# First loads of the input projection in eighths on two queues, the norm's broadcast matmuls behind three quarters of a column tile, ScalarE's table loaded ahead

## The chip, the cores and the metric

One core of a Trainium2 chip runs the whole program. The metric is device time in microseconds (us) of one execution, the median over several. TensorE (PE) multiplies matrices into PSUM, VectorE (DVE), ScalarE (ACT) and GpSimd (POOL) work elementwise, SyncE (SP) issues most of the DMAs. All data are f32.

## The reference, cut to what matters

One layer of a decoder for 512 prompt tokens and 8 sample tokens, 520 in all. The change is at its very beginning:

```python
def _rmsnorm(x, g):
    y = x * lax.rsqrt(jnp.mean(x * x, axis=-1, keepdims=True) + EPS) * g
    return y
def _layer(...):
    a = _rmsnorm(h, norm_mix)          # h: 520 x 1024
    proj = a @ w_in                    # w_in: 1024 x 1800: pooling, gate z, x/B/C, dt
    v_pool, z, xbc, dt_raw = proj[..., :o1], proj[..., o1:o2], proj[..., o2:o3], proj[..., o3:]
    pool_out, new_pool = _pool_mixer(v_pool, ...)
    ssd_out, new_conv, new_ssm = _ssd_mixer(z, xbc, dt_raw, ...)
    h = h + concat([pool_out, ssd_out]) @ w_out
    h = h + _hier_moe(_rmsnorm(h, norm_ffn), ...)      # 32 experts, two of them per token
    gate = sigmoid(_rmsnorm(h, norm_ple) @ ple_gate_w + ple_gate_b)
    h = h + gate * (p @ ple_proj_w)
# output: _rmsnorm(h, norm_final), and the new pooling, conv and SSD states
```

## The kernel before

The program is written by hand, engine by engine: each engine's block is a list of instructions in the order in which they run, with semaphore waits (`wait_ge`) between engines. Nothing is scheduled by a tool. `Steps` and `last` are helpers that count an engine's own semaphore.

**The input projection** multiplies the 1024 model dimensions, in 8 slices (k) of 128, by column tiles of 128 outputs. The host has transposed the tokens (`xT`, 128 x 8 x 520) and sorted the columns of `w_in`: `w_a` holds the first four tiles (`A_TILES` 4, 5, 0, 1 of x/B/C), `w_b` dt and two more, `w_v` the pooling tiles, `w_z` the gate's. `aproj(j, k0, k1)` (line 598) is tile j of the first four over some slices: two matmuls per slice, one for each half of the tokens (128x260), so 16 per tile. An f32 matmul stands as two records in the trace (32 per tile). These four tiles start before the norm is known: VectorE only multiplies xT by the norm's gains (line 1551, into `xg`, one instruction per slice, which `aproj(0, ...)` waits for), and the inverse root of each token is multiplied in when the tile leaves PSUM (`take_a`, lines 1567 to 1569).

**The inverse roots** take a path of their own. ScalarE squares and sums the untransposed rows `h1` (line 1116, five tiles of rows, each behind its own load `ld_x`, all behind the constants `ld_const`), GpSimd adds eps and takes the power -0.5 (lines 1405 and 1406, `inverse_root`), VectorE puts the roots on a diagonal (line 1557, `rdiag`), TensorE multiplies ones by it (line 652, five matmuls) so that every partition holds all 520 roots, and VectorE copies them out of PSUM banks 4 and 5 (lines 1559 and 1560, `rstd_b`, semaphore `s_rb_out`). Tile 3 of `aproj` writes the same banks, so it waits for `s_rb_out`.

TensorE's order there is: tiles 0 and 1, slice by slice together as the four quarters land (lines 645 to 648), the five broadcast matmuls, tile 2, tile 3, then dt (`dtproj`, lines 616 and 619), which needs `aT`, the tokens with gain and root in them (line 1585, eight instructions, `s_aT_ready`). Then come the transposes of the sample's conv state and pooling state (line 593 and 667, behind `ld_state`), and tile by tile the rest of the projection (`inproj`, line 633) between the SSD mixer's matmuls. VectorE's order beside that is: `take_a(0)`, `take_a(1)`, `aT`, `take_a(2)`, two convolutions (line 1576), `take_a(3)`, and the chain from the raw dt to its cumulated sums (lines 1595 to 1609, `s_acs_ready`), for which TensorE waits at line 678.

**The loads.** SyncE issues in this order (lines 467 to 494): four times a quarter of xT (two slices, 520 KB) and a quarter of w_a (512 KB), the constants (380 KB), five tiles of `h1` rows, w_b, w_v, w_z, the SSD states, two copies in DRAM. ScalarE issues the vectors (`vec`, 37 KB: gains and biases), GpSimd the two small states (lines 1395 and 1396). Each has a semaphore of its own. The first expert weights are issued by SyncE when the mixer's output is there (`s_mix_ready`, line 516), and later ones as TensorE frees their buffers.

## Time and profile before

| what | value |
|---|---|
| time, median of 3 runs | 569.43 us (569.17, 569.43, 572.87) |
| time of the profiled execution | 570.61 us |
| its span, first to last instruction | 568.8 us |
| mean granted TensorE clock | 0.965 |
| PE busy | 507.8 us (89%) |
| DVE, ACT, POOL busy | 207.7, 154.1, 111.8 us |
| DMA | 144.72 MB, mean 254 GB/s |

Times in the profile are counted from the first instruction. The profiled execution lies 1.8 us around its span, and 1.2 us above the median. An engine that is busy is not for that reason the bound: a row of the waits or of the timeline says, in brackets, how long an engine stood idle before an instruction and which instruction or DMA released it. SPq, ACTq and PEq are the engines' sequencers, which issue DMAs.

### The profile page before, as it was taken

To read this page: it belongs to the slowest core of one execution; us is meant where nothing else is said; L and a number is where in the kernel's file an instruction comes from. 1 tells how busy PE (TensorE), PEld (TensorE's weight loads), DVE (VectorE), ACT (ScalarE), POOL (GpSimd) and SP (SyncE) were. 2 spreads that over 40 slices of the span, in tenths; PEclk is the share of its full clock that TensorE was granted. 3 is DMA by queue.
4 is the path that set the end of the run, shared out by engine and by line. 5 is a ranking of instruction groups with operands and counts; after the bars stand their busy time and mean duration, and the time that the engine had idled before them with its cause. 6 is when DMAs were issued, how large, how long until landed. Compare 5 with 4: busy or idle time off the path is not lost.

```text
span 568.8 us, 7815 instructions
## 1 busy us (share of the span) xinstructions
PE 507.8 (89%) x3098; PEld 312.2 (55%) x3098; DVE 207.7 (37%) x496; ACT 154.1 (27%) x315; POOL 111.8 (20%) x178
## 2 busy tenths in 40 slices
PE   5899999999999997199999999978776999999994
PEld 4688886768645554165555555544343554344443
DVE  1286496523033546432221121111110211169455
ACT  0435163103534121102222222211210223355223
POOL 1200048993001001101121111111011223022001
PEclk9999999999999999579999999999996999999999
DMA  8990000503449705949999999999999999640001
GB/s 290 418 295 3 1 1 10 213 1 68 170 163 400 328 9 199 414 142 341 418 417 415 416 417 416 414 416 417 416 413 382 413 413 365 217 196 39 3 37 74
DMA packets 40214, 144.72 MB, mean 254 GB/s; under 512 B 14522, under 2 KB 15162, under 8 KB 31076
## 3 DMA queue, kind: packets, MB, share of 16 engines
q1 hardware_dynamic: 33316, 132.79, 59.4%
q0 software_dynamic: 5152, 8.85, 4.2%
q10 hardware_dynamic: 1712, 2.62, 1.2%
q8 instruction: 23, 0.38, 0.3%
q14 instruction: 11, 0.09, 0.0%
HBM read 140.15 MB, written 14.19 MB: 271 GB/s over the span
## 4 chain that ended last, share of the span: by engine, by line
PE 44%; DMA 10%; DVE 3%; issue 2%; SPq 2%; ACT 1%; POOLq 0%; POOL 0%; DVEq 0%; ACTq 0%
PE PS L989 18%; PE PS L1092 10%; PE PS L1010 9%; DMA mem<-in_exp_w_down 5%; PE PS L593 4%; DVE mem L1878 2%; DMA u_rows<-mem 2%; DMA mem<-u_rows,idx_all 1%; DMA choice_rows<-mem,out_i 1%; DMA mem<-choice_rows 1%; SPq L484 1%; PE PS L834 1%; SPq L486 1%; PE PS L990 1%; PE PS L996 1%
## 5 line engine op out<-in xcount | busy, mean ns | idle before, releaser
L989 PE MATMUL PS<-mem 128*64 128x256 f32 x512 | 119.3, 387 | 6.8 <-DVE mem L1878 6.8
L990 PE MATMUL PS<-mem 128*64 128x256 f32 x512 | 119.3, 387 | 0.0
L989 PEld LDWEIGHTS PS<-mem 128*64 128x64 f32 x512 | 68.4, 139 | 43.2 <-DVE mem L1878 7.6
L1010 PE MATMUL PS<-mem 128*64 128x512 f32 x256 | 62.6, 610 | 18.1 <-issue 9.0
L633 PE MATMUL PS<-mem 128*128 128x260 f32 x320 | 73.3, 385 | 0.0
L990 PEld LDWEIGHTS PS<-mem 128*64 128x64 f32 x512 | 68.4, 139 | 0.0
L633 PEld LDWEIGHTS PS<-mem 128*128 128x128 f32 x320 | 59.8, 190 | 10.5 <-issue 1.5
L1882 DVE TENSOR_TENSOR mem<-PS,mem 64x256 f32<-64x256 f32 x32 | 13.7, 428 | 119.6 <-ACT mem L1288 119.6
L821 PE MATMUL PS<-mem 128*128 128x512 f32 x128 | 56.6, 595 | 0.0
L1092 PE MATMUL PS<-mem 128*128 128x512 f32 (+1 forms) x144 | 56.1, 547 | 0.0
L593 PEld LDWEIGHTS PS<-mem 128*128 128x128 f32 (+4 forms) x254 | 31.0, 170 | 45.5 <-issue 29.9
L593 PE MATMUL PS<-mem 128*128 128x128 f32 (+4 forms) x254 | 40.0, 289 | 13.5 <-DMA mem<-u_rows,idx_all 12.5
L1878 DVE TENSOR_TENSOR mem<-PS,mem 128x512 f32<-128x512 f32 x34 | 23.5, 692 | 75.3 <-PE PS L593 75.2
L1288 ACT ACTIVATE mem<-PS 64x256 f32<-64x256 f32 x32 | 12.0, 375 | 134.5 <-PE PS L990 134.5
L1010 PEld LDWEIGHTS PS<-mem 128*64 128x64 f32 x256 | 18.4, 139 | 43.6 <-issue 31.6
L1092 PEld LDWEIGHTS PS<-mem 128*128 128x128 f32 x144 | 27.0, 190 | 26.3 <-issue 25.5
L1405 POOL TENSOR_TENSOR mem<-mem 128x1 f32<-128x1 f32 (+1 forms) x20 | 4.5, 225 | 175.9 <-ACT mem L1256 85.2
L821 PEld LDWEIGHTS PS<-mem 128*128 128x128 f32 x128 | 23.8, 190 | 26.9 <-issue 26.8
L604 PE MATMUL PS<-mem 128*128 128x260 f32 x128 | 31.6, 412 | 6.8 <-DMA mem<-in_w_a 6.8
L1293 ACT ACTIVATE mem<-PS 64x512 f32<-64x512 f32 x32 | 18.9, 590 | 65.3 <-PE PS L1010 65.3
L604 PEld LDWEIGHTS PS<-mem 128*128 128x128 f32 x128 | 26.3, 207 | 11.3 <-DMA mem<-in_w_a 6.8
L1483 POOL DMA_INDIRECT mem<-u_rows,idx_all x15 | 15.3, 1021 | 79.4 <-PE PS L593 70.5
(270 smaller groups left out, 547.4 us busy)
## 6 DMA issues: line engine op xcount, KB each, us to landing
mem<-in_exp_w_down SPq DMA_DIRECT2D x32, 1024.0 KB, 21.2
mem<-in_exp_w_gate SPq DMA_DIRECT2D x32, 1024.0 KB, 18.9
mem<-in_exp_w_up SPq DMA_DIRECT2D x32, 1024.0 KB, 22.0
mem<-in_w_out SPq DMA_DIRECT2D x2, 2048.0 KB, 7.4
mem<-in_ple_gate_w SPq DMA_DIRECT2D x1, 4096.0 KB, 29.7
mem<-choice_rows SPq DMA_DIRECT2D x4, 1024.0 KB, 8.8
mem<-in_xT SPq DMA_DIRECT2D x4, 520.0 KB, 9.1
mem<-in_w_a SPq DMA_DIRECT2D x4, 512.0 KB, 9.9
```

What stands on the lines that cost most here:

```text
L593: return pe.transpose(dst, src, ident[0:n, 0:n])
L604: ins = pe.matmul(PS[A_BANKS[j][h]][:, 0:HALF], COLS[j][2][:, k, :], xg[k // 4][:, k % 4, h * HALF:(h + 1) * HALF], start=(k == 0), stop=( ...
L633: ins = pe.matmul(PS[b + h][:, 0:HALF], w[:, k, :], aT[:, k, h * HALF:(h + 1) * HALF], start=(k == 0), stop=(k == KT - 1))
L821: return pe.matmul(PS[OUT_BANKS[i][h]][:, :], mix_col(k, ORDER[i]), w_out[:, k, h * 512:(h + 1) * 512], start=(k == 0), stop=(k == KT - 1))
L989: pe.matmul(PS[0][0:S, 0:FF], rows_k, gu[slot][:, k, :], start=(k == 0), stop=(k == KT - 1))
L990: ins = pe.matmul(PS[1][S:2 * S, 0:FF], rows_k, gu[slot][:, KT + k, :], start=(k == 0), stop=(k == KT - 1))
L1010: ins = pe.matmul(PS[4 + h][h * S:(h + 1) * S, :], actT[:, s % 2, f * S:(f + 1) * S], dn[slot][:, f, h * 512:(h + 1) * 512], start=(f == 0 ...
L1092: ins = pe.matmul(PS[4 if q else 2 * (i % 2) + h][:, 0:w], uTr[:, i % 2, k * P:(k + 1) * P], w_ple[:, k, h * 512 + q * w:h * 512 + (q + 1) ...
L1293: A(ysb[rows, s // 2, 0:512], PS[4][0:S, :], ACT.Copy)
L1483: pool.indirect_dma_start(G[:, q, :], None, u_dram, bass.IndirectOffsetOnAxis(ap=idx, axis=0), bounds_check=TOK - 1, oob_is_err=False).the ...
L1878: tt(uT[:, slot, half * 512:half * 512 + 512].rearrange("p (k c) -> p k c", c=P), tiles(PS[6 + half][:, :]), g_ffn[:, 4 * half:4 * half + ...
L1882: tt(act_tok[:, s % 2, :], PS[1][S:2 * S, 0:FF], sg[:, s % 2, :], ALU.mult).then_inc(s_act_ready, 1)
```

## The change

- The first loads are cut in five pieces instead of four: slice 0, slice 1, and then three pairs (`FIRST_K`). xT is issued by SyncE, w_a by ScalarE, behind `vec`.
- ScalarE takes one Square of a 128x1 column as soon as `vec` has landed, which brings its table load to that place.
- TensorE puts slices 0 to 5 of tile 2 ahead of the five broadcast matmuls, and slices 6 and 7 behind them.
- GpSimd issues the two small states behind the first inverse root instead of at its start.
- Three loads share a semaphore with another, with the count adapted: the last prompt rows and the sample rows, and w_v and w_z.

```diff
--- before.py
+++ after.py
@@ -27,6 +27,7 @@
 ROWS = [128, 128, 128, 128, NS]
 TAIL = [0, 4, 1, 2, 3]
 ORDER = [0, 1, 4, 2, 3]
+FIRST_K = [(0, 1), (1, 2), (2, 4), (4, 6), (6, 8)]
 OUT_BANKS = [(2, 3), (0, 1), (2, 2), (0, 1), (2, 3)]
 NL = 40
 PP_BANKS = [0, 1, 2, 3, 0, 1, 2, 3, 0, 1]
@@ -449,10 +450,10 @@
         st_out = sem("st_out")
         st_shift = sem("st_shift")
         ld_vec = sem("ld_vec")
-        ld_xT = [sem(f"ld_xT{i}") for i in range(4)]
-        ld_wa = [sem(f"ld_wa{i}") for i in range(4)]
-        ld_x = [sem(f"ld_x{i}") for i in range(NT)]
-        ld_w = [sem(f"ld_w{i}") for i in range(3)]
+        ld_xT = [sem(f"ld_xT{i}") for i in range(len(FIRST_K))]
+        ld_wa = [sem(f"ld_wa{i}") for i in range(len(FIRST_K))]
+        ld_x = [sem(f"ld_x{i}") for i in range(NT - 1)]
+        ld_w = [sem(f"ld_w{i}") for i in range(2)]
         w_full = [sem(f"w_full{i}") for i in range(NGU)]
         d_full = [sem(f"d_full{i}") for i in range(NDN)]
         g_full = [sem(f"g_full{i}") for i in range(2)]
@@ -464,17 +465,15 @@
         @block.sync
         def _(sp):
 
-            for i in range(4):
-                kk = slice(2 * i, 2 * i + 2)
-                sp.dma_start(xg[i // 2][:, 2 * (i % 2):2 * (i % 2) + 2, :], a["xT"][:, kk, :]).then_inc(ld_xT[i], 16)
-                sp.dma_start(w_a[:, kk, :], a["w_a"][:, kk, :]).then_inc(ld_wa[i], 16)
+            for i, (k0, k1) in enumerate(FIRST_K):
+                sp.dma_start(xg[k0 // 4][:, k0 % 4:k0 % 4 + k1 - k0, :], a["xT"][:, k0:k1, :]).then_inc(ld_xT[i], 16)
             sp.dma_start(const, a["consts"]).then_inc(ld_const, 16)
             for t in range(NT):
                 src = a["x_prompt"][0, t * P:(t + 1) * P, :] if t < 4 else a["x_sample"][:, 0, :]
-                sp.dma_start(h1[0:ROWS[t], t, :], src).then_inc(ld_x[t], 16)
+                sp.dma_start(h1[0:ROWS[t], t, :], src).then_inc(ld_x[min(t, 3)], 16)
             sp.dma_start(w_b, a["w_b"]).then_inc(ld_w[0], 16)
             sp.dma_start(w_v, a["w_v"]).then_inc(ld_w[1], 16)
-            sp.dma_start(w_z, a["w_z"]).then_inc(ld_w[2], 16)
+            sp.dma_start(w_z, a["w_z"]).then_inc(ld_w[1], 16)
             for t in range(4):
                 sp.dma_start(hs[:, t].rearrange("p (b n) -> p b n", n=NST),
                              a["state_ssm"][0, :, 2 * t:2 * t + 2].rearrange("b h p n -> (h p) b n")
@@ -623,7 +622,7 @@
                 w = COLS[j][2]
                 b = 2 * (j % 2)
                 if k0 == 0:
-                    pe.wait_ge(ld_w[0 if j < J_V else 1 if j < J_Z else 2], 16)
+                    pe.wait_ge(ld_w[0 if j < J_V else 1], 16 if j < J_V else 32)
                     if j == J_X:
                         pe.wait_ge(s_a_out, 2)
                     else:
@@ -642,17 +641,18 @@
             def chunk_rows(c):
                 return acs[DTP * c:DTP * c + DTP, :]
 
-            for part in range(4):
+            for part, (k0, k1) in enumerate(FIRST_K):
                 pe.wait_ge(ld_wa[part], 16)
                 for j in range(2):
-                    aproj(j, 2 * part, 2 * part + 2)
+                    aproj(j, k0, k1)
+            aproj(2, 0, 6)
             for t in range(NT):
                 R = ROWS[t]
                 pe.wait_ge(s_rdiag_ready, t + 1)
                 ins = pe.matmul(PS[4 + t // 4][:, (t % 4) * P:(t % 4) * P + R], ones[0:R, :], rdiag[0:R, t, 0:R],
                                 start=True, stop=True)
             ins.then_inc(s_rb_done, 1)
-            aproj(2, 0, KT)
+            aproj(2, 6, KT)
             pe.wait_ge(s_rb_out, 1)
             aproj(3, 0, KT)
 
@@ -1108,11 +1108,15 @@
             step = Steps(act, own_act)
             A = act.activation
             act.dma_start(vec, a["vec"]).then_inc(ld_vec, 16)
+            for i, (k0, k1) in enumerate(FIRST_K):
+                act.dma_start(w_a[:, k0:k1, :], a["w_a"][:, k0:k1, :]).then_inc(ld_wa[i], 16)
+            act.wait_ge(ld_vec, 16)
+            A(ss[:, 20:21], vec[:, 0:1], ACT.Square)
             root_d = 1.0 / D ** 0.5
 
             act.wait_ge(ld_const, 16)
             for t in range(NT):
-                act.wait_ge(ld_x[t], 16)
+                act.wait_ge(ld_x[min(t, 3)], 16 if t < 3 else 32)
                 A(junk[0:ROWS[t], :], h1[0:ROWS[t], t, :], ACT.Square, scale=root_d,
                   accum_out=ss[0:ROWS[t], t:t + 1]).then_inc(s_squares, 1)
                 act.wait_ge(s_squares, t + 1)
@@ -1392,8 +1396,6 @@
         @block.gpsimd
         def _(pool):
             step = Steps(pool, own_pool)
-            pool.dma_start(sconv, a["state_conv"][0].rearrange("b r c -> (b r) c")).then_inc(ld_state, 16)
-            pool.dma_start(spool, a["state_pool"][0].rearrange("b r c -> (b r) c")).then_inc(ld_state, 16)
 
             step(pool.memset(idle[:, :], 0.0))
             pool.memset(dtw[0], 0.0)
@@ -1409,6 +1411,9 @@
                 R = ROWS[t]
                 pool.wait_ge(s_squares, t + 1)
                 inverse_root(R, t, ss[0:R, t:t + 1], eps[0:R, :], s_inverse_root)
+                if t == 0:
+                    pool.dma_start(sconv, a["state_conv"][0].rearrange("b r c -> (b r) c")).then_inc(ld_state, 16)
+                    pool.dma_start(spool, a["state_pool"][0].rearrange("b r c -> (b r) c")).then_inc(ld_state, 16)
 
             pool.wait_ge(s_states_in, 1)
             pool.wait_ge(s_inproj_out, 3)
@@ -1546,8 +1551,9 @@
 
             dve.wait_ge(ld_vec, 16)
             for k in range(KT):
-                if k % 2 == 0:
-                    dve.wait_ge(ld_xT[k // 2], 16)
+                for i, (k0, k1) in enumerate(FIRST_K):
+                    if k == k0:
+                        dve.wait_ge(ld_xT[i], 16)
                 ts(xg[k // 4][:, k % 4, :], xg[k // 4][:, k % 4, :], vec[:, V_MIX + k:V_MIX + k + 1], None, ALU.mult).then_inc(s_xg_ready, 1)
 
             dve.wait_ge(ld_const, 16)
```

How the rows stand on the engines' lists. SyncE, before: its first DMAs.

```order
L469 DMA mem<-in_xT 128x1040
L470 DMA mem<-in_w_a 128x1024
L469 DMA mem<-in_xT 128x1040
L470 DMA mem<-in_w_a 128x1024
L469 DMA mem<-in_xT 128x1040
```

ScalarE at its start, the changed program (`in_vec` the vectors, `in_w_a` the first weights):

```order
L1110 DMA mem<-in_vec 128x74
L1112 DMA mem<-in_w_a 128x512 x2
L1112 DMA mem<-in_w_a 128x1024 x3
L1114 ACT_TABLE_LOAD
L1114 ACTIVATE mem<-mem 128x1
L1120 ACTIVATE mem<-mem 128x1024 x4
L1120 ACTIVATE mem<-mem 8x1024
```

The five loads of w_a have come to ScalarE's list, in front of the table load, which stands on its own now and no longer at the first Square of 1024 columns.

TensorE from its start, before (the first group is `aproj`, L652 the broadcast of the roots, L616 the dt columns):

```order
L604 MATMUL PS<-mem 128x260 x32
L652 MATMUL PS<-mem 128x128 x4
L652 MATMUL PS<-mem 128x8
L604 MATMUL PS<-mem 128x260 x32
L616 MATMUL PS<-mem 32x128 x32
```

and in the changed program:

```order
L603 MATMUL PS<-mem 128x260 x44
L652 MATMUL PS<-mem 128x128 x4
L652 MATMUL PS<-mem 128x8
L603 MATMUL PS<-mem 128x260 x20
L615 MATMUL PS<-mem 32x128 x32
```

Twelve matmuls (24 records) have moved from behind the broadcast to the front of it; their number is unchanged.

GpSimd, the changed program, where the inverse roots begin (before, the two DMAs stood ahead of all its memsets):

```order
L1407 TENSOR_TENSOR mem<-mem 128x1
L1408 TENSOR_TENSOR mem<-mem 128x1
L1415 DMA mem<-in_state_conv 24x768
L1416 DMA mem<-in_state_pool 120x512
L1407 TENSOR_TENSOR mem<-mem 128x1
```

The second root now stands behind two DMA issues.

## Rows read from the trace of the kernel before

**Rows 1.** The windows, a long stretch after the start: busy us by engine, clock, DMA.

```profile
core 0: us, PE busy (x) PEld busy (x) DVE busy (x) ACT busy (x) POOL busy (x), PEclk, DMA share, GB/s
60.00:163.00 103.00, 101.16 (x626) 76.11 (x625) 49.32 (x103) 35.66 (x74) 50.24 (x64) 1.00 0.20 64
```

**Rows 2.** The timeline, TensorE: start us, us, line, op, count, [idle <- releaser].

```profile
6.80 15.86 PE L604 MATMUL PS<-mem 128*128 128x260 f32 x64 [6.80 <-DMA mem<-in_w_a]
22.50 0.45 PE L652 MATMUL PS<-mem 128*128 128x128 f32 x2
27.52 15.75 PE L604 MATMUL PS<-mem 128*128 128x260 f32 x64
43.19 1.95 PE L616 MATMUL PS<-mem 128*32 128x128 f32 x64
```

**Rows 3.** The windows, around the start and the broadcast (columns as in rows 1).

```profile
0.00:4.00 4.00, 0.00 (x0) 0.00 (x0) 0.00 (x0) 0.00 (x0) 1.97 (x10) 1.00 0.55 173
4.00:6.00 2.00, 0.00 (x0) 0.00 (x0) 0.89 (x2) 0.00 (x0) 0.00 (x0) 1.00 0.94 234
6.80:10.00 3.20, 3.20 (x8) 2.52 (x9) 0.11 (x1) 0.00 (x0) 0.00 (x0) 1.00 1.02 311
10.00:13.20 3.20, 3.20 (x16) 2.79 (x15) 1.46 (x4) 0.00 (x0) 0.00 (x0) 1.00 1.03 413
27.10:30.50 3.40, 3.40 (x9) 2.80 (x10) 2.85 (x9) 1.15 (x2) 0.00 (x0) 0.50 1.00 419
30.50:43.20 12.70, 12.70 (x59) 10.73 (x59) 9.59 (x18) 3.73 (x5) 0.00 (x0) 1.00 0.90 265
```

**Rows 4.** The timeline, ScalarE, GpSimd and VectorE on the inverse roots.

```profile
18.67 1.28 ACT L1116 ACT_TABLE_LOAD   x1 [18.67 <-DMA mem<-in_x_prompt]
19.96 1.06 ACT L1116 ACTIVATE mem<-mem 128x1024 f32<-128x1024 f32 x1
22.37 0.19 POOL L1405 TENSOR_TENSOR mem<-mem 128x1 f32<-128x1 f32 x1 [0.36 <-ACT mem L1116]
22.64 0.55 POOL L1406 TENSOR_TENSOR mem<-mem 128x1 f32<-128x1 f32 x1
26.74 0.22 DVE L1557 TENSOR_SCALAR mem<-mem 8x8 f32<-8x8 f32 x1 [0.87 <-POOL mem L1406]
```

**Rows 5.** The timeline, VectorE's first work and GpSimd's two issues.

```profile
4.52 0.89 DVE L1551 TENSOR_SCALAR mem<-mem 128x520 f32<-128x520 f32 x2 [4.52 <-DMA mem<-in_vec]
1.27 0.74 POOL L1395 DMA_DIRECT2D mem<-in_state_conv  x1 [0.86 <-POOLq L2019]
2.02 0.58 POOL L1396 DMA_DIRECT2D mem<-in_state_pool  x1
```

**Rows 6.** The timeline, TensorE in one stretch at full clock, and around the state transposes.

```profile
35.65 7.62 PE L604 MATMUL PS<-mem 128*128 128x260 f32 x34
58.20 0.39 PE L683 MATMUL PS<-mem 128*128 128x128 f32 x2
58.51 0.64 PE L686 MATMUL PS<-mem 8*64 8x17 f32 x16
```

**Rows 7.** The timeline, VectorE behind the broadcast.

```profile
27.62 0.69 DVE L1559 COPY mem<-PS 128x512 f32<-128x512 f32 x1 [0.66 <-PE PS L652]
29.90 4.96 DVE L1585 TENSOR_TENSOR mem<-mem 128x520 f32<-128x520 f32 x8
37.10 4.56 DVE L1576 SCALAR_TENSOR_TENSOR mem<-mem 128x512 f32<-128x512 f32 x6
52.31 0.28 DVE L1609 TENSOR_SCALAR mem<-mem 128x128 f32<-128x128 f32 x1
59.20 0.63 DVE L1612 COPY mem<-PS 128x452 f32<-128x452 f32 x1 [4.36 <-PE PS L686]
```

**Rows 8.** The DMA view: two loads with KB and us from issue to landing.

```profile
mem<-in_state_pool POOLq DMA_DIRECT2D x1, 240.0 KB, 8.2
mem<-in_pool_lin_w ACTq DMA_DIRECT2D x1, 256.0 KB, 9.7
```

## The prediction

> **What bounds the kernel now.** I read the page, then the windows, then the timeline of the first 60 us engine by engine. TensorE is the bound: it is busy 89% of the span, and from 60 to 163 us 101.16 of 103 us [rows 1]. The stretches in which it later waits for expert weights begin with DMAs that are themselves issued when TensorE's mixer work is done (the front's semaphore `s_mix_ready`), so they move with it. What TensorE gains in the first 60 us should therefore reach the end, unless another engine takes over on the way.
>
> TensorE's beginning has three losses. It starts at 6.80 us, when the first quarter of w_a lands. It then runs its first two tiles in 15.86 us. Between 22.66 (6.80 + 15.86) and 27.52 us it does no tile work: five short matmuls, each waiting for a root [rows 2]. And it is slow twice. From 27.10 to 30.50 the granted clock is 0.50, the lower level of 1.2 GHz, after those five broken-up microseconds; the records of a tile come 9 in 3.4 us there and 59 in 12.7 us after it. In the first 3.2 us 8 records come, and 16 in the next 3.2, so the first microseconds run at the lower level too, though the clock column shows 1.00 there [rows 3].
>
> **Term 1, the spread broadcast.** Twelve matmuls of tile 2 (24 records) go ahead of it. At full clock 34 records take 7.62 us, and the last one's tail is some 0.4, so a record costs (7.62 - 0.4)/33 = 0.22 us [rows 6], and 24 cost 5.3. If TensorE ended tiles 0 and 1 where it does now, it would come to the broadcast at 22.66 + 5.3 = 28.0; the last root stands on the diagonal at 26.74 + 0.22 = 26.96 [rows 4]. With a start 1.7 us earlier (term 3) it comes at 26.3. The roots come earlier as well: the table load of 1.28 us leaves the front of the first Square [rows 4], which brings them to 25.7 with unchanged landings. The last rows behind it should land sooner too, as 312 KB of states no longer stand ahead of them. GpSimd now issues two DMAs behind root 0, 0.74 + 0.58 = 1.3 us [rows 5]. A Square of 1.06 us comes each 1.2 us with what lies around it, and a root costs 0.8 (22.37 to 22.64 + 0.55) [rows 4], so GpSimd is late by 0.9, 0.5, 0.1 us for roots 1 to 3 and on time for root 4. Nobody waits in that line for the middle ones.
>
> What stays is the five matmuls back to back. As they stand, two records take 0.45 us [rows 2], 2.3 in all; a 128-column matmul in a dense stretch takes 0.31 (58.20 to 58.51) [rows 6], which gives 1.5, and the fifth has only 8 columns. I take 1.2. The break of 27.52 - 22.66 = 4.86 us then shrinks to 1.2: gain 3.7, with 2.6 and 3.9 as ends. VectorE's copies of the roots (0.69 us and a short one [rows 7]), for which tile 3 waits, have slices 6 and 7 of tile 2 as their cover: 4 matmuls, 8 records, 1.75 us.
>
> **Term 2, the clock behind it.** Tiles 2 and 3 take 15.75 us [rows 2]; at 0.22 per record 64 records take 63 x 0.22 + 0.4 = 14.2. With no break there is nothing for which the clock should fall: gain 1.5, with 0 and 1.7 (half of the 3.4 us) as ends.
>
> **Term 3, the start.** Now 520 + 512 KB of the first quarters and the 37 KB of vectors must land. After the change it is the first eighth of xT (260 KB) with the vectors beside it on ScalarE's queue, then w_a's first (256 KB) beside the second eighth of xT: about 813 KB before the first product. ScalarE issues it second, as SyncE did with the quarter. In the first 4 us 173 GB/s flow on average, 0.7 MB, and 234 GB/s after that [rows 3], so the last of 813 KB have moved by 4.5. The quarters and vec, 1069 KB with what of the states comes between, would by the same rates be through at about 5.7 to 6, and the product starts at 6.80; a landing thus follows by some 0.7 or more: 5.1 to 5.3 us. VectorE needs vec, which lands at 4.52 now, and 0.45 us for its first slice (0.89 for two) [rows 5]: 5.0. So TensorE starts at about 5.1, 1.7 earlier. After that the data stay ahead: at the lower clock a slice of both tiles costs 8 records x 0.43 = 3.5 us and at the higher one 1.75, against 516 KB that arrive in 1.2 us at 413 GB/s and in 2.2 at 234 [rows 3]; two or three slices are stored up by the time the clock rises.
>
> The gain is smaller than the 1.7 if the clock still rises at 10.0 us: the extra 1.7 us are then worked at half rate and give 0.85. If it rises 3.2 us after the start, as now, they give the whole 1.7. Nothing in the trace decides this. I take 1.3; the ends are 0.4 (start at 6.4, w_a being held up as now) and 2.0.
>
> The Trainium skill, "TensorE: Matmul & The Clock Gate", section "Part 1: The HAM clock gate (the 'warmup' mystery)", says that the lower clock is the default and activity releases it, at a point that varies from run to run. By that, the trace agrees in the slow first 8 records, and a part of term 3 may come or fail by execution; by the page alone the sum keeps either end.
>
> **What costs nothing, and by which cover.** ScalarE's five issues of w_a and its tiny Square stand before 18.67 us, when it now begins at all [rows 4]. TensorE asks for the two states behind dt, which will end at about 39 us; issued at about 20 they have 18 us, and the larger took 8.2 [rows 8]. The joint semaphore of w_v and w_z is asked for behind the matmuls at 58.2 [rows 6], some 52 then; the 11.8 MB up to and with w_z take 29 to 38 us at 413 to 311 GB/s [rows 3]. The new issue place on GpSimd is counted above. Losing the covers would cost at most 1.3 us for GpSimd.
>
> **Who is late next.** TensorE reaches dt 6.5 us earlier, at 36.7 instead of 43.19 [rows 2]. VectorE has its copies of the roots at 27.62 now [rows 7], and at 26.3 + 1.2 = 27.5 then, so it is hardly earlier: aT is ready at 34.7 instead of 29.90 + 4.96 = 34.9, still before TensorE. Its two convolutions (4.56 us [rows 7]) then follow take_a(2) without a wait, and take_a(3) comes at about 40 instead of 43.3 (27.52 + 15.75); the dt chain behind it, which ends with 52.31 + 0.28 [rows 7], ends at about 49. TensorE asks for that result now at 58.20 [rows 6], then at 51.7: 2.7 us of room. VectorE waits 4.36 us for TensorE at 59.20 [rows 7] and meets it there again. So the whole gain passes.
>
> **Sum.** 3.7 + 1.5 + 1.3 = 6.5 us. From the profiled execution, 570.61 - 6.5 = 564.1. The median of the runs lies 1.2 us below that execution: 569.43 - 6.5 = 562.9 us.
>
> **Rivals.**
>
> A. *The start brings little.* ScalarE's queue and SyncE's share the same DMA engines, and two queues add no bandwidth. For it: between 4 and 6 us only 234 GB/s flow though the DMA engines are busy at 0.94 [rows 3]. Against it: fewer bytes are asked before the first product. Then term 3 is 0.4 and the sum 5.6: 563.8. The Trainium skill, "DMA: Bandwidth & Descriptors", section "Issuing engines are not separate DMA queues", says the same: issuing on several engines saves issue time alone. By that rule the split itself gives nothing, and the smaller first pieces and the states' absence carry term 3.
>
> B. *VectorE takes over.* If its chain to the dt sums does not come forward at all, TensorE waits before L683 until 52.6 + 0.1, against 58.20 now: 5.5 us pass, 563.9. For it: VectorE has next to no pause from 27.62 to 34.9 and from 37.10 to 41.7 [rows 7]. Against it: the room of 2.7 us.
>
> C. *Slower: w_a starves on ScalarE's queue.* A load of 256 KB that ScalarE issues beside SyncE's big ones takes 9.7 us to land [rows 8], which is 26 GB/s. w_a with the vectors is 2085 KB. Tiles 0 and 1 need the last slices by about 17 us; the terms 1 and 2 of 5.2 us are eaten up when both tiles end 5.2 us late, at 27.9, which is a last landing at 24.4 us: 2085 KB in 22.5 us, 93 GB/s. Below that rate the kernel is slower, at 60 GB/s (last landing at 37 us) by some 12 us: 582. For it: rows 8. Against it: that load beside w_z goes in rows of 512 bytes against 16 KB ones, while w_a's rows of 2 and 4 KB stand against the same sizes of xT, so both queues should get half.
>
> D. *The rows land late, as xT, w_a and they now share the DMA engines in another order:* the broadcast waits between its matmuls, term 1 is at its low end and the clock falls behind it as now. 2.6 + 0 + 1.3 = 3.9, 565.5. For it: three of the five loads of rows are behind more traffic of another queue. Against it: the last root has 0.6 us of room even by today's landings.
>
> **How the numbers follow.** Forecast 0.60, A 0.15, B 0.10, D 0.12, C 0.03. A measurement of this kernel tells about 1% (5.7 us) from no change, so faster by over 1% is a time below 563.7. The forecast's own spread (term 1 up to 3.9, term 2 up to 1.7, term 3 up to 2.0: 7.6, 561.8) lies mostly below it, A about at it, B and D above: 0.66 faster, 0.31 same, 0.03 slower. The range reaches from 560.9 (all high ends, and 0.9 for what differs from run to run) to 565.8 (case D and a little).
>
> **What would show it right or wrong.** Right: first product at about 5.1 us; one block of 88 records, the five broadcast matmuls within 1.5 us and without a wait for VectorE; no stretch at 0.50 near 27 us; dt at about 36.7; VectorE's wait at the tri copy smaller than 4.36 us but there. Wrong: waits for w_a inside the first block; a clock of 0.50 behind the broadcast; TensorE waiting at L683 or for aT; a gain at 60 us that is gone at 163.

## The result, and the profile after

The changed kernel takes 566.92 us in the median of 8 runs (564.46 to 568.11), the kernel before 570.63 (569.17 to 572.87) beside it. The ratio is 0.9925, with a 95% interval of 0.990 to 0.9951: 4.3 us gained by the ratio, 0.75% (the plain difference of the two medians is 3.7). Run again beside other runs of before, it came to 0.9897 (0.9869 to 0.9926), 5.9 us; the two intervals overlap from 0.990 to 0.9926. The prediction had 562.9 us and a range from 560.9 to 565.8: the direction was right, the size too large.

The profiled execution took 567.58 us against 570.61 before: 3.0 us gained in that pair. "Lead" below is how much earlier than in the profile of before the same instruction comes. TensorE at its start, after (the timeline; start us, us, line, op, count, [idle before <- releaser]; beside [rows 2]):

```profile
5.70 5.50 PE L603 MATMUL PS<-mem 128*128 128x260 f32 x16 [5.70 <-DMA mem<-in_w_a]
11.60 16.05 PE L603 MATMUL PS<-mem 128*128 128x260 f32 x72 [0.41 <-DMA mem<-in_w_a]
27.48 1.37 PE L652 MATMUL PS<-mem 128*128 128x128 f32 x10
28.78 9.04 PE L603 MATMUL PS<-mem 128*128 128x260 f32 x40
37.74 1.96 PE L615 MATMUL PS<-mem 128*32 128x128 f32 x64
```

The reader sees both halves of the change. The broadcast of the roots (L652) stands as one block, from 27.48 to 28.78 before tile work goes on, without a wait. The dt columns start at 37.74 instead of 43.19: 5.45 us earlier. But the first block has a wait for w_a in it, which was not there before; the 16 records of slices 0 and 1 end at 11.2, and the third piece of w_a lands at 11.6.

The roots and VectorE behind them, after (the timeline; [rows 4] and [rows 7]):

```profile
17.19 1.06 ACT L1120 ACTIVATE mem<-mem 128x1024 f32<-128x1024 f32 x1 [11.81 <-DMA mem<-in_x_prompt]
25.14 0.22 DVE L1563 TENSOR_SCALAR mem<-mem 8x8 f32<-8x8 f32 x1 [0.87 <-POOL mem L1408]
28.89 0.69 DVE L1565 COPY mem<-PS 128x512 f32<-128x512 f32 x1 [3.53 <-PE PS L652]
53.75 0.63 DVE L1618 COPY mem<-PS 128x452 f32<-128x452 f32 x1 [1.74 <-PE PS L686]
```

The last root is on the diagonal at 25.4, 2.1 us before TensorE asks for the first. VectorE's wait at the tri copy (the last line) shrank from 4.36 to 1.74 us and is still there, so VectorE takes nothing from TensorE.

How far the 5.45 us carry is seen at SyncE's issues of later weights (`w_out`, the experts' gate weights), which wait for TensorE's work. Before:

```profile
146.82 0.38 SPq L514 DMA_DIRECT2D mem<-in_w_out  x1
436.70 0.33 SPq L484 DMA_DIRECT2D mem<-in_exp_w_gate  x1
443.84 0.33 SPq L484 DMA_DIRECT2D mem<-in_exp_w_gate  x1
```

and after:

```profile
141.36 0.38 SPq L513 DMA_DIRECT2D mem<-in_w_out  x1
431.74 0.33 SPq L483 DMA_DIRECT2D mem<-in_exp_w_gate  x1
440.85 0.33 SPq L483 DMA_DIRECT2D mem<-in_exp_w_gate  x1
```

The lead is 5.46 us at 147, 4.96 at 437 and 2.99 at 444, and 3.0 at the end. Nearly 2 us go within 7. The windows show why; first before, from TensorE's restart behind a wait for expert weights to the rise of its clock, then the same stretch after (columns as in [rows 1]):

```profile
431.50:436.70 5.20, 5.16 (x15) 1.98 (x15) 0.39 (x1) 1.18 (x2) 0.17 (x2) 0.50 0.87 348
```

```profile
426.60:435.90 9.30, 9.30 (x34) 4.49 (x36) 0.98 (x2) 1.18 (x2) 1.56 (x4) 0.50 0.93 374
```

TensorE restarts 5 us earlier, but the clock rises at 435.9 instead of 436.7. It works 9.3 us at the lower level (1.2 GHz) where it had worked 5.2, and half of the difference is 2.0 us. Whether that is the change's doing or an execution's luck is one of the questions below.

### The profile page after: what moved, and what is told of

The parts are those of the page before. It is cut to its first block, busy times and chain, and to the rows that moved or that the text cites. A ratio compares the mean times of both kernels' runs of the same rounds, so it can differ in the third digit from the quotient of the medians.

```text
span 565.7 us, 7819 instructions
## 1 busy us (share of the span) xinstructions
PE 510.3 (90%) x3098; PEld 313.3 (55%) x3098; DVE 207.6 (37%) x496; ACT 154.0 (27%) x316; POOL 111.4 (20%) x178
## 4 chain that ended last, share of the span: by engine, by line
PE 46%; DMA 8%; SPq 3%; DVE 2%; issue 1%; ACT 0%; POOLq 0%; POOL 0%; DVEq 0%; ACTq 0%
PE PS L989 18%; PE PS L1092 10%; PE PS L1010 9%; DMA mem<-in_exp_w_down 5%; PE PS L592 4%; PE PS L935 3%; DVE mem L1884 2%; DMA u_rows<-mem 2%; DMA mem<-u_rows,idx_all 1%; SPq L483 1%; SPq L485 1%; SPq L489 1%; PE PS L834 1%; PE PS L990 1%; PE PS L1002 0%
## 5 line engine op out<-in xcount | busy, mean ns | idle before, releaser
L989 PE MATMUL PS<-mem 128*64 128x256 f32 x512 | 121.7, 393 | 6.8 <-DVE mem L1884 6.8
L990 PE MATMUL PS<-mem 128*64 128x256 f32 x512 | 121.7, 393 | 0.0
L989 PEld LDWEIGHTS PS<-mem 128*64 128x64 f32 x512 | 69.6, 141 | 44.5 <-DVE mem L1884 7.5
L990 PEld LDWEIGHTS PS<-mem 128*64 128x64 f32 x512 | 69.6, 141 | 0.0
L592 PE MATMUL PS<-mem 128*128 128x128 f32 (+4 forms) x254 | 40.2, 291 | 13.1 <-DMA mem<-u_rows,idx_all 12.3
L1010 PEld LDWEIGHTS PS<-mem 128*64 128x64 f32 x256 | 18.6, 140 | 42.2 <-issue 30.3
L603 PEld LDWEIGHTS PS<-mem 128*128 128x128 f32 x128 | 25.2, 199 | 10.7 <-DMA mem<-in_w_a 6.7
```

Source lines behind the costliest of these rows:

```text
L592: return pe.transpose(dst, src, ident[0:n, 0:n])
L603: ins = pe.matmul(PS[A_BANKS[j][h]][:, 0:HALF], COLS[j][2][:, k, :], xg[k // 4][:, k % 4, h * HALF:(h + 1) * HALF], start=(k == 0), stop=( ...
L989: pe.matmul(PS[0][0:S, 0:FF], rows_k, gu[slot][:, k, :], start=(k == 0), stop=(k == KT - 1))
L990: ins = pe.matmul(PS[1][S:2 * S, 0:FF], rows_k, gu[slot][:, KT + k, :], start=(k == 0), stop=(k == KT - 1))
L1010: ins = pe.matmul(PS[4 + h][h * S:(h + 1) * S, :], actT[:, s % 2, f * S:(f + 1) * S], dn[slot][:, f, h * 512:(h + 1) * 512], start=(f == 0 ...
```

## The experiments

At TensorE's start the clock column shows 1.00 throughout, so its level is read off the records of `aproj`: one each 0.43 us at the lower clock, one each 0.22 at the higher. "Slow" is the time from the first product until they come at the full pace, "dt" the start of the dt columns (43.19 before, 37.74 after). A single execution of the changed kernel falls anywhere within 3.6 us, so an experiment with one run is read by its profile's head, and its time ranks nothing.

**1. The spread broadcast alone.** Onto the kernel before:

```diff
-            for t in range(NT):
+            aproj(2, 0, 6)
+            for t in range(NT):
...
-            aproj(2, 0, KT)
+            aproj(2, 6, KT)
```

> The kernel before with one part of the change: slices 0 to 5 of tile 2 ahead of the broadcast of the roots. Theory: nearly all of the gain at the head comes from here, the loads give next to nothing. The dt columns, which start at 43.19 us before and at 37.74 after, start at 43.19 - 5.2 = 38.0 (37.8 to 38.5), TensorE starts at 6.80 and the clock does not fall near 27 us. The time lies within 1 us of the changed kernel's. Rival: without the earlier table load the roots are late for the broadcast (last root at about 27.0, TensorE there at 22.5 + 5.2 = 27.7 by the records), the five matmuls wait and the clock falls: dt at 39.5 or later. Second rival: the loads carry the gain after all: dt at 40 or later.

Measured: 566.57 us (6 runs), ratio 0.9926 (0.9897 to 0.9955), as the changed kernel's first ratio: by the time alone, nothing beyond the spread is resolved. TensorE:

```profile
6.70 22.60 PE L604 MATMUL PS<-mem 128*128 128x260 f32 x88 [6.70 <-DMA mem<-in_w_a]
29.14 1.37 PE L653 MATMUL PS<-mem 128*128 128x128 f32 x10
30.43 9.03 PE L604 MATMUL PS<-mem 128*128 128x260 f32 x40
39.40 1.95 PE L616 MATMUL PS<-mem 128*32 128x128 f32 x64
```

dt at 39.40 is later than expected, but neither for a wait at the broadcast nor for a fall of the clock. The slow beginning was longer, as the windows say:

```profile
6.70:12.90 6.20, 6.20 (x14) 4.88 (x15) 1.21 (x3) 0.00 (x0) 0.00 (x0) 1.00 1.02 362
12.90:16.00 3.10, 3.10 (x16) 2.67 (x15) 1.42 (x4) 0.00 (x0) 0.00 (x0) 1.00 1.02 407
```

14 records in 6.2 us, then 16 in 3.1; before, it was 8 in 3.2 and then 16 in 3.2 [rows 3]. The 3 us more at half rate cost 1.5 us. Without that, dt would stand at 37.9 and the lead be 5.3: the expected 5.2. So terms 1 and 2 of the prediction are shown at their size, and the profile that it was made from held, by luck, a slow beginning at the short end of what the profiles show (3.2 to 6.2 us without a warm-up).

**2. The loads alone.** In the changed kernel the broadcast goes back ahead of all of tile 2 (the diff of 1 in reverse).

> The changed kernel with the broadcast put back ahead of all of tile 2; loads, states and table load stay as changed. Theory: TensorE starts at 5.7 and both first tiles end at about 22.2, 0.3 earlier than before; the roots are ready at 19.6 to 25.4, so the broadcast waits until about 25.4 instead of 27.2, which the earlier rows and the table load give: tile 2 starts at about 25.7 and the clock falls or not by luck; dt starts at 41.4 if it falls as before, 39.9 if it does not. Rival (loads give nothing at all): dt at 43.

Measured: 567.05 us (one run). TensorE:

```profile
22.42 0.83 PE L651 MATMUL PS<-mem 128*128 128x128 f32 x6
23.82 0.49 PE L651 MATMUL PS<-mem 128*128 128x128 f32 x2 [0.57 <-DVE mem L1562]
25.22 14.29 PE L603 MATMUL PS<-mem 128*128 128x260 f32 x64
39.45 1.95 PE L615 MATMUL PS<-mem 128*32 128x128 f32 x64
```

Three of the five roots are there when TensorE comes; it breaks for 2.6 us instead of 4.9, tile 2 starts at 25.2, and the clock does not fall behind that (14.29 us for 64 records, against 15.75). dt at 39.45 is a lead of 3.7 us, by 0.45 us beyond the 39.9 expected without a fall, since tile 2 starts half a microsecond sooner than thought. At the end of tiles 0 and 1 the lead is only 0.1 us (22.58 against 22.67). So the earlier rows of tokens, which bring the roots, do most of what the spread does, in another way, and the gains do not add up: 5.3 and 3.7 give 5.45 together.

**3 and 4. One queue.** w_a goes back to SyncE, in turn with xT, in the same five pieces; once with a single run and once timed.

```diff
             for i, (k0, k1) in enumerate(FIRST_K):
                 sp.dma_start(xg..., a["xT"][:, k0:k1, :]).then_inc(ld_xT[i], 16)
+                sp.dma_start(w_a[:, k0:k1, :], a["w_a"][:, k0:k1, :]).then_inc(ld_wa[i], 16)
...
-            for i, (k0, k1) in enumerate(FIRST_K):
-                act.dma_start(w_a[:, k0:k1, :], a["w_a"][:, k0:k1, :]).then_inc(ld_wa[i], 16)
```

> The changed kernel with w_a issued by SyncE in turn with xT again, piece by piece (two eighths, then pairs). Theory of turns by packet: xT runs ahead of w_a since ScalarE's 2 KB packets take turns with SyncE's 4 KB ones; in one queue both arrive in step. First product at 5.2 to 5.7 us, the second eighth of w_a landed by about 7.0 instead of 9.0, no wait for w_a between 9 and 12 us (0.41 us at 11.60 after), dt at 37.2 to 37.5 instead of 37.74. Rival (the DMA rate of about 300 GB/s between 4 and 8 us limits it, whatever the queue): waits for w_a as after, dt within 0.1 of 37.74.

> The changed kernel with w_a issued by SyncE in turn with xT, timed. One look showed the first product at 4.51 us and the dt columns 6.95 us earlier than before, but only 3.64 us at the end, where the clock stayed at 0.50 for long twice. Theory of luck: over several executions the median gains 6 to 7 us on before, 564.0 to 565.0. Rival (something after the head takes whatever exceeds about 4 us): 566.5 to 567.5, no better than the changed kernel.

Measured: 566.98 us in the single run, 564.01 timed (6 runs, 563.17 to 566.53), ratio 0.9888 (0.9852 to 0.9923). The timed one's TensorE:

```profile
4.55 21.89 PE L604 MATMUL PS<-mem 128*128 128x260 f32 x88 [4.55 <-DMA mem<-in_w_a]
26.28 1.37 PE L653 MATMUL PS<-mem 128*128 128x128 f32 x10
36.54 1.96 PE L616 MATMUL PS<-mem 128*32 128x128 f32 x64
```

The first product comes at 4.55 us (4.51 in the single run), more than a microsecond ahead of the changed kernel's 5.70 and earlier than the 5.2 to 5.7 expected, and TensorE does not wait for w_a after it: the third piece lands at 10.1 and 10.4 us in the two executions, 11.6 in the changed kernel. The second eighth landed at 7.5 and 7.8, not by 7.0 as expected. The second queue, which was part of the change, costs. The two profiles differ by 0.3 us at dt (36.25 and 36.54) and by 3.6 us in the span (565.1 and 561.5). Most of what lies between is the clock, as the window from 426 to 436 us shows, first in the single run, then in the timed execution:

```profile
426.00:436.00 10.00, 10.00 (x40) 4.96 (x42) 0.98 (x2) 1.18 (x2) 1.56 (x4) 0.53 0.93 371
```

```profile
426.00:436.00 10.00, 9.87 (x60) 5.11 (x57) 1.52 (x4) 2.33 (x5) 1.57 (x4) 0.85 0.95 381
```

The median of 564.01 lies at the lower end of the range expected. The rival of experiment 4, that something after the head takes what exceeds about 4 us, had 566.5 to 567.5 and falls.

**5. All pieces of one slice, on two queues.**

```diff
-                sp.dma_start(xg..., a["xT"][:, k0:k1, :]).then_inc(ld_xT[i], 16)
+                for k in range(k0, k1):
+                    sp.dma_start(xg[k // 4][:, k % 4, :], a["xT"][:, k, :]).then_inc(ld_xT[i], 16)
...
-                act.dma_start(w_a[:, k0:k1, :], a["w_a"][:, k0:k1, :]).then_inc(ld_wa[i], 16)
+                for k in range(k0, k1):
+                    act.dma_start(w_a[:, k, :], a["w_a"][:, k, :]).then_inc(ld_wa[i], 16)
```

The waits of TensorE and VectorE count 16 * (k1 - k0) accordingly.

> The changed kernel with every piece of xT and w_a a single slice, so that packets of 2080 bytes stand against 2048 on the two queues (the pairs wait for two DMAs on one semaphore). Theory of turns by packet: both queues now get half of the bytes, the second eighth of w_a lands at about 7.5 instead of 9.0, no wait at 11.60; first product at 5.7 as after; dt at 37.2 to 37.5. Rival (rate): as after, dt within 0.1 of 37.74; smaller packets may even cost.

Measured: 565.11 us (one run), dt at 37.95, and the wait for w_a is gone: 88 records from 5.64 in 22.21 us without a break. The DMA view from 5 to 8 us shows how the two queues share (q1 SyncE's, q10 ScalarE's; packets, MB, share of the 16 engines). The changed kernel:

```profile
q1 hardware_dynamic: 165, 0.62, 62.2%
q10 hardware_dynamic: 153, 0.31, 35.1%
```

and with slices of equal size:

```profile
q10 hardware_dynamic: 265, 0.48, 51.8%
q1 hardware_dynamic: 254, 0.47, 43.6%
```

The queues take turns by packet: in both kernels about as many packets each, whatever their size. In the changed kernel SyncE has come to the pairs of xT (rows of 4160 bytes) while ScalarE still sends eighths (2048 bytes), so w_a gets a third of the bytes just when TensorE needs it. With equal pieces it gets half, and it lands earlier: the second eighth at 8.1 us instead of 9.0, the third piece at 11.0 instead of 11.6. The theory holds in these shares and landings. At dt nothing of it is shown: dt did not come earlier than 37.74, for the slow beginning lasted 5.4 us here and 3.5 there, and that a late clock hides the wait by itself is seen in experiment 12, where the changed kernel with a slow beginning of 6.0 us has no wait either. With half of the slow time taken off, dt is 35.2 in both. The first product comes at 5.64, as in the changed kernel, where the pieces up to there are single slices as well; the size of the packets does not explain its 1.1 us behind one queue.

**6 and 7. Quarters, in one queue and on two.** In experiment 3's kernel and in the changed kernel:

```diff
-FIRST_K = [(0, 1), (1, 2), (2, 4), (4, 6), (6, 8)]
+FIRST_K = [(0, 2), (2, 4), (4, 6), (6, 8)]
```

> The changed kernel with the loads as before the change (quarters, xT and w_a in turn on SyncE's queue), so without cut and without second queue; states, table load and spread broadcast as changed. Theory: the first product comes when 1069 KB have landed, without the states beside them at about 6.2 to 6.6 us instead of 6.80, against 4.5 with the eighths in one queue: the cut is worth about 2 us, and the second queue costs 1.2. No wait for w_a in the first block; dt at 37.5 to 39.5 by the luck of the clock's rise. Rival (the states' absence gave the early start, not the cut): first product at 5 or earlier.

> The changed kernel with quarters in place of the cut, on two queues. Theory of turns by packet: packets of 4160 and 4096 bytes stand against each other, but the second quarter of xT flows beside the first of w_a, so that some 1.56 MB move before the first product: it comes at 7.2 to 7.8 us, later than in one queue (6.2 to 6.6) and later than before (6.80). Rival (the queues do not matter, only the bytes asked for): within 0.2 of the one-queue version.

Measured: 565.97 and 567.54 us (one run each). One queue:

```profile
6.59 22.04 PE L604 MATMUL PS<-mem 128*128 128x260 f32 x88 [6.59 <-DMA mem<-in_w_a]
```

Two queues:

```profile
8.61 21.79 PE L603 MATMUL PS<-mem 128*128 128x260 f32 x88 [8.61 <-DMA mem<-in_w_a]
40.49 1.95 PE L615 MATMUL PS<-mem 128*32 128x128 f32 x64
```

So the cut into eighths is worth 2.0 us of the first product in one queue (6.59 to 4.55) and 2.9 on two (8.61 to 5.70), and the second queue costs 2.0 with quarters and 1.15 with eighths. The absence of the states gives 0.1 to 0.2 at the first product (6.70 or 6.80 to 6.59). With quarters the cost was larger than expected, 8.61 against 7.2 to 7.8; why by so much stays open.

**8. The states early.** In the changed kernel GpSimd's two loads go back to its start.

> The changed kernel with GpSimd's loads of the two states put back at its start. Theory: their 312 KB flow between 5 and 10 us and slow the loads of w_a: the first product stays at 5.7 or comes at 6, the third piece of w_a lands at 12.0 to 12.8 instead of 11.5, so the wait in the first block grows from 0.41 us to 0.9 to 1.7, and dt comes that much later (38.2 to 39.0). Rival (the states cost nothing there): all as after, dt 37.74 but for the point at which the clock rises.

Measured: 568.14 us (one run).

```profile
5.95 3.78 PE L603 MATMUL PS<-mem 128*128 128x260 f32 x8 [5.95 <-DMA mem<-in_w_a]
9.91 2.02 PE L603 MATMUL PS<-mem 128*128 128x260 f32 x8 [0.18 <-DMA mem<-in_w_a]
12.62 16.05 PE L603 MATMUL PS<-mem 128*128 128x260 f32 x72 [0.69 <-DMA mem<-in_w_a]
```

Two waits of together 0.87 us instead of 0.41, the third piece lands at 12.6 instead of 11.6, and dt comes at 38.77, 1.0 later. Moving the states is worth 1 us of dt in this pair of profiles.

**9. Without the early table load.** In the changed kernel:

```diff
-            act.wait_ge(ld_vec, 16)
-            A(ss[:, 20:21], vec[:, 0:1], ACT.Square)
```

> The changed kernel without the small Square that brings the table load ahead. Theory: the roots come 1.28 us later (last on the diagonal at 25.36 + 1.28 = 26.6 us), still before TensorE asks for the first of them at 27.2 to 27.5; dt stays at 37.7 but for the point at which the clock rises (37.2 to 39). Rival (the broadcast waits): idle time of TensorE for VectorE between 26 and 29 us and more than 1.4 us for the broadcast.

Measured: 564.84 us (one run), dt at 37.91, no wait at the broadcast. The last root was on the diagonal at 25.6, not 26.6:

```profile
25.40 0.22 DVE L1561 TENSOR_SCALAR mem<-mem 8x8 f32<-8x8 f32 x1 [0.71 <-POOL mem L1406]
```

In the changed kernel ScalarE waits 1.00 us before its fourth Square, for the sample's rows: the last prompt rows share their semaphore since the change. With the table load in front of the first Square, at 17.32, all five run back to back and the delay is taken up by that wait, down to 0.3 us. So the part is worth 0.3 us on the last root, which nobody waits for.

**10. A pad in the head.** In the changed kernel, in front of the dt columns:

```diff
+            pe.wait_ge(s_a_out, 1)
+            for _ in range(12):
+                pe.matmul(PS[0][:, 0:HALF], w_a[:, 0, 0:P], xg[0][:, 0, 0:HALF], start=True, stop=True)
             dtproj()
```

> The changed kernel with 12 more matmuls of 128x260 in front of the dt columns, which TensorE works back to back: 24 records of 0.22 us, 5.2 us, so that its head ends where it ended before (dt shift -5.45 + 5.2 = -0.25 in the profile). It asks whether what is gained at the head reaches the end. Theory: yes, and the 1 to 2 us that the profiled execution lost later are luck of the clock: the median is that of the changed kernel plus 5.2, about 572, and ratio to before 1.000 to 1.003. Rival: the stretches that are bound by weight transfers absorb a part of any gain at the head: then the pad costs less than it takes, 2.5 to 4.3 us, 569.5 to 571.

Measured: 570.62 us (12 runs), ratio 1.0003 (0.9982 to 1.0024). The pad took 5.4 us and dt came at 42.68, half a microsecond ahead of before:

```profile
37.33 5.42 PE L662 MATMUL PS<-mem 128*128 128x260 f32 x24
42.68 1.95 PE L615 MATMUL PS<-mem 128*32 128x128 f32 x64
```

With the head where it was, the time is where it was. Against the changed kernel's two ratios (0.9925 and 0.9897) the pad costs 4.5 and 6.1 us, around the 5.2 to 5.4 that it takes. The median itself, 570.62, was expected at about 572 and lies in the rival's 569.5 to 571: it is 3.7 us above the changed kernel's first median and 5.1 above its second. With an interval of 1.2 us to either side for the pad's ratio alone, the times do not separate the two. What separates them is the lead at fixed instructions, in the part on why the prediction was wrong.

**11. A warm-up.** Onto the one-queue version, seven matmuls of zeros while the first loads are under way:

```diff
+            pe.wait_ge(s_pads, 1)
+            for _ in range(7):
+                pe.matmul(PS[7][:, 0:P], dtw[0][:, 0:P], dtw[0][:, 0:P], start=True, stop=True)
             for part, (k0, k1) in enumerate(FIRST_K):
```

> The one-queue version with seven 128x128 matmuls of zeros on an unused PSUM bank from about 1.3 us on, while the first loads are under way (nothing that they write is used). Theory: the slow first microseconds of TensorE, 8 records or more at half rate behind the first product, are what its clock takes to rise after it has begun to work; work that begins 3 us earlier brings the rise to between 4.5 and 8 us instead of 8 to 12, first product unchanged at 4.5 to 4.8, dt columns 1 to 2 us earlier than with one queue alone; median 562.5 to 564. Rival: the rise is not moved by such small matmuls, or comes no earlier than about 8.5 us; then dt and median are those of one queue, perhaps 0.3 later as the warm-up overruns.

Measured: 563.72 us (6 runs), ratio 0.9882 (0.9847 to 0.9917), not to be told from the one-queue version's 0.9888.

```profile
1.27 3.36 PE L647 MATMUL PS<-mem 128*128 128x128 f32 x14 [1.27 <-POOL mem L1405]
4.68 4.91 PE L604 MATMUL PS<-mem 128*128 128x260 f32 x16
10.12 16.05 PE L604 MATMUL PS<-mem 128*128 128x260 f32 x72 [0.53 <-DMA mem<-in_w_a]
```

It does what it was meant to: the first 16 records take 4.91 us instead of the one-queue version's 5.8 and 6.1, and the clock rises 1.7 us behind the first product instead of 4.1 and 4.7. Then TensorE has used up slices 0 and 1 at 9.6 and waits for the third piece, which lands at 10.1. Neither theory nor rival had that: behind a faster clock the loads are the bound, and what is left at dt is 0.3 us against one execution of the one-queue version (36.27 against 36.54) and nothing against the other (36.25).

**12. The changed kernel again.**

> The changed kernel itself once more, to narrow its ratio to before beside the one-queue version's 0.9888. Theory: head gain of 5.5 us (profile) less or more by luck of the clock, 0.990 to 0.9935; the one-queue version stays the faster by 1 to 2 us. Rival (the two are the same and the ratio of 0.9925 was bad luck): 0.9885 to 0.990.

Measured: 565.51 us (6 runs, 563.99 to 567.71), ratio 0.9897 (0.9869 to 0.9926). TensorE in its profile:

```profile
5.60 22.50 PE L603 MATMUL PS<-mem 128*128 128x260 f32 x88 [5.60 <-DMA mem<-in_w_a]
```

dt is at 38.20, the slow beginning lasts 6.0 us, and there is no wait for w_a: the first 16 records end at 12.3, and the third piece lands at 11.6 as before. The ratio lies in the rival's range (0.9885 to 0.990) and just outside the theory's (0.990 to 0.9935); its interval holds both, so this does not decide between them. One queue's 0.9888 is 0.5 to 2.1 us better by the ratios, with intervals that overlap: that it is the faster is shown only at the head.

Head of all that have the spread and the late states, by what differs:

| kernel | first product | slow | dt |
|---|---|---|---|
| after | 5.70 | 3.5 | 37.74 |
| after, again | 5.60 | 6.0 | 38.20 |
| all eighths, two queues | 5.64 | 5.4 | 37.95 |
| one queue, two executions | 4.51, 4.55 | 4.1, 4.7 | 36.25, 36.54 |
| quarters, one queue | 6.59 | 5.1 | 38.73 |
| quarters, two queues | 8.61 | 4.5 | 40.49 |
| after, without the early table load | 5.80 | 4.2 | 37.91 |
| after, with the pad (its start for dt) | 5.79 | 3.4 | 37.33 |

## Why the prediction was wrong

**Terms 1 and 2 were right.** Together they were put at 5.2 us. In the profiled pair TensorE's 64th record stands 0.28 us earlier than before and dt 5.45: 5.17 us come from the broadcast and the clock behind it. The broadcast takes 1.30 us (forecast 1.2), and the clock does not fall. Experiment 1 has them alone, at 5.3 once half of the longer slow beginning is taken off.

**Term 3 is the step that failed.** It was put at 1.3 us and came to 0.28 at the end of tiles 0 and 1. It failed in two places.

The first is the start: TensorE began 1.1 us earlier than before, at 5.70, where 1.7 had been forecast (5.1). The bytes were counted about rightly: at the measured 178 GB/s over the first 4.6 us, 813 KB have moved by then, and one queue, where 553 KB suffice, has its first product at 4.5. What was too small is the time from there to the landing: 0.6 us in the forecast, 1.0 as measured. The rows of before had held it: the forecast itself put its bytes at 5.7 to 6 for a start at 6.80, which is 0.8 to 1.1.

The second is "after that the data stay ahead". It compares rates, and the pieces of w_a were late because xT's larger packets had gone beside them: TensorE had used up slices 0 and 1 at 11.2, and with the wait for the third piece and the slower first records behind it lost 0.67 us. The slow beginning of 3.5 instead of 3.2 us took the other 0.15. In the changed kernel's second profile the slow beginning of 6.0 us took the place of the wait.

The landing of the pieces of w_a after (issues, then us to landing):

```profile
L1112 ACTq DMA_DIRECT2D mem<-in_w_a x5: 440/453/732, 1.2 to 3.1; - x5
DMA to landing us min/median/max: 4.5/9.4/13.3
```

The last piece, issued at 3.1, lands at 16.4. Rival A had the right sign and place (0.4 for the start), and part of its reason. It leaned on the Trainium skill ("DMA: Bandwidth & Descriptors", section "Issuing engines are not separate DMA queues"), by which a second issuing engine saves only issue time. The trace agrees in the main: over the first 8.6 us the mean rate is 245 GB/s in the changed kernel and 234 in one queue, with quarters 249 and 252. But the second queue also cost 1.15 to 2.0 us of the first product. The same page of the Trainium skill, section "Queues, rings and completion order", says that each DMA engine goes round the queues by packet; the trace agrees (153 packets beside 165, with half the bytes).

**Who is late next** was read rightly: VectorE keeps a wait of 1.74 us, smaller than 4.36 but there, as forecast, and TensorE waits neither at L683 nor for aT (rival B). **The covers** held, and the table load turned out to be needless rather than hidden. Rival C (w_a starves) has its mechanism in small, a third of the bytes for 3 us, and not its price. Rival D (the rows land late) did not come: the first rows are there for ScalarE at 17.2 us instead of 18.7.

**"So the whole gain passes" held for the kernel and not for the profile.** The lead can be followed through every profile at the same issues of gate weights (us before the same issue in the profile of before; the times in the head are before's):

| kernel | dt | at 219.61 | at 250.63 | at 436.70 | at 443.84 | end |
|---|---|---|---|---|---|---|
| after | 5.45 | 5.46 | 4.92 | 4.96 | 2.99 | 3.0 |
| after, again | 4.99 | 5.01 | 5.13 | 5.02 | 5.02 | 4.8 |
| one queue, single run | 6.94 | 6.96 | 5.65 | 5.57 | 3.59 | 3.6 |
| one queue, timed | 6.65 | 6.65 | 7.11 | 7.27 | 7.28 | 7.3 |
| spread alone | 3.79 | 3.78 | 3.92 | 4.13 | 4.09 | 4.1 |
| states early | 4.42 | 4.43 | 4.27 | 4.20 | 2.46 | 2.5 |
| pad | 0.51 | 0.51 | 0.71 | 0.80 | 0.80 | 0.8 |

In all 13 profiles the lead at dt is there at 219.61 to within 0.05 us, so nothing absorbs it on the way. Between these points and 436.70, where the experts' weights bound the kernel, it swings by up to some 2 us from issue to issue and comes back. What stays changes at two places: by -1.3 to +0.9 us across the routing, and by 1.7 to 2.0 us between 437 and 444 in the three profiles that take the long way at the lower clock, by less than 0.15 in the others. One kernel, the changed one, has both behaviours, and so has the one-queue version, and the largest lead (7.27) is kept whole; so the loss goes with the execution and not with the size of the lead. What makes the clock rise late in one execution and not in another is not shown.

The times fall into groups in the same way. Of the changed kernel's own 8 runs four have a mean clock of 0.958 and take 567.4 to 568.1, and four of 0.963 to 0.970 take 564.5 to 566.5; of the second set one of 6 is at 0.958. The one-queue version shows the same two groups (563.2 to 564.7 and 566.4 to 566.5). The kernel before has them too: 18 of the 37 runs of it beside the experiments are at 0.959 or lower.

**The base was read off too few runs.** The median of before was 569.43 with 3 runs and 570.63 with 8, 570.8 to 571.6 in later sets. The forecast gain of 6.5 from 570.63 would have been 564.1. Of the 4.0 us by which the forecast missed, 1.2 are the base and 1.0 is term 3. The remaining 1.8 are not traced to a step. Four of the eight executions took the long way, but the base's median holds such executions as well; and in the second set the medians lie 6.1 us apart (571.62 and 565.51), where 6.5 less 1.0 would be 5.5, so nothing is missing there. The 1.8 is about what two timings of one kernel differ by (1.4 us in the median, 1.6 by the ratio). The range allowed 0.9 for what differs from run to run.

## What to carry to other kernels

When two loads are needed in step, put them in one queue in the order of need. On two queues they took turns by packet here, so that the larger packets of one pushed back the smaller of the other, and pieces that were not needed yet flowed beside those that were. Cut the first pieces small (worth 2.0 us of the first product in one queue) and keep other loads out of the first microseconds. And where the clock's rise differs by execution, compare the leads at a fixed instruction, subtract half of what ran slow, and take the base from many runs before a range is set.

## What was not expected of the hardware

The time that TensorE needs at its start until its records come at full pace is not fixed: 3.2 us in the profile before, 3.5 and 6.0 in two profiles of the same changed kernel, 6.2 in experiment 1. Each microsecond of it costs half. The same holds behind long waits (5.2 and 9.3 us at 0.50 around 430). The Trainium skill ("TensorE: Matmul & The Clock Gate", Part 1) says that this differs from run to run; it was cited, and the sum still used the one value of the profile.

Between 4 and 6 us the DMA engines move far below the 410 GB/s of later, with or without the states beside them: 234 [rows 3], 296 in the changed kernel, 220 in one queue. From 8 to 10 us it is 395 to 427 in the versions without the states, and 301 to 320 in the three profiles with them. Why the first microseconds are slow in every version stays open.
